# Attention of a hybrid decoder step: sample value products over four column groups, V pages from two queues, logits in pairs

## The chip, the cores and the metric

The kernel runs on one core of a Trainium2 chip. The metric is the device time of one execution in microseconds. A core has TensorE (PE, with its weight loads shown as PEld), VectorE (DVE), ScalarE (ACT), GpSimd (POOL) and SyncE (SP, which here only issues transfers). PSUM is the memory that TensorE writes, in banks of 512 fp32 numbers per partition.

## The reference

One step of a two-layer decoder: 512 prompt tokens and 8 sample tokens share all weights. Layer 0 is a gated MLP mixer, layer 1 is sparse attention, and each is followed by a channel mixer that looks up experts by key. The change touches layer 1's attention alone. In it, every query keeps the best keys by an index score and attends to these only:

```python
def _sparse_attend(q, qi, wi, ki_all, q_pos, n_keep, gather_kv):
    s = jax.nn.relu(jnp.einsum('bthd,bsd->bths', qi, ki_all))
    score = jnp.einsum('bths,bth->bts', s, wi).astype(jnp.float32) * IDX_SCALE
    ...
    _, idx = lax.top_k(score, n_keep)
    k_sel, v_sel = gather_kv(idx)
    logits = jnp.einsum('bthgd,btnhd->bthgn', qg, k_sel).astype(jnp.float32) * (HEAD_DIM ** -0.5)
    ...
    prob = jax.nn.softmax(logits, axis=-1).astype(v_sel.dtype)
    o = jnp.einsum('bthgn,btnhd->bthgd', prob, v_sel)
```

The prompt has 512 keys (16 query heads, 4 KV heads, head dimension 64). Each of the 8 samples has 2048 past keys in 16 pages of 128, found by a page table, and one new key. A V page is 128 rows of 256 fp32 numbers, 128 KB.

## The kernel before

The program has a hand-written instruction stream for each engine, with semaphores between them; nothing is moved by a scheduler. The order in which TensorE's code is written is the order in which it issues.

Attention (`attention` in TensorE's stream, line 789) goes through these stages: projections (line 818), index scores of the prompt (`index_of`, line 834) together with K pages and logits of the samples (line 845), the search for the samples' cutoff (lines 896 to 898, driven by DVE), transposes of the samples' probabilities into `pT_s` and `pnewT` (lines 902 to 910), and then the prompt's attention with the samples' value products between its steps (line 973). Then come the output projection `ao` and the second channel mixer.

The prompt's attention has 64 items, item i being head i % 16 of query block i // 16. Block b has b + 1 blocks of 128 keys. Per item TensorE computes logits (`log_of`, line 936) into one of two banks of `acc`; DVE adds the mask and takes the maximum into `prob` (`biased`, line 2008); ScalarE takes the exponential (`exp_of`, line 1365); TensorE transposes it (`turn`, line 948); ScalarE copies it to `probT` (`take_turned`, line 1373); TensorE multiplies with V (`pv`, line 959); DVE scales the result (`output`, line 2024). TensorE's loop does the logits of item i, the transposes of item i - 2 and the product of item i - 3 in one turn. After the last product of a block, `block_output` (line 968) transposes it, and ScalarE and DVE split it into a high and a low part.

After every odd item there is one value step `s_values(k)` (line 914): sample b, pages 4u to 4u + 3. Its four matmuls have 32 columns of `pT_s` as weights and a page of V as the moving operand (256 columns). Sample b writes partitions 32 (b % 4) to 32 (b % 4) + 31 of one bank, so the four matmuls of a step write the same 32 partitions. After sample b's last step one matmul (line 926) adds the new token's value. There are 32 steps.

SP issues all 128 V pages (line 533), four per buffer `unit`, each after the step that last used the buffer, and reads each page number from `table` into a register. The K pages went through the same four buffers before, issued by SP and ScalarE. Each weight slab of the dense stages is loaded by SP into `raw`, split by ScalarE into `w_hi` and by GpSimd or DVE into `w_lo`. While the prompt's attention runs, GpSimd does nothing; four slabs of `ao` are loaded already.

GpSimd loads the 13 constants of the attention (line 2141) before its part of the norm (line 2083).

## Time and profile before

| | us |
|---|---|
| median of 3 runs | 3879.66 |
| lowest and highest of the 3 | 3871.08 and 3888.6 |
| span of the profiled execution | 3870.3 |
| TensorE busy | 3639.7 |
| VectorE busy | 2458.9 |
| GpSimd busy | 1814.7 |
| ScalarE busy | 1356.3 |

The profile is one execution. Its page gives the busy time of each engine and the costliest groups; the trace behind it can be asked for waits, for the instructions of a stretch in order of time, and for the busy time of each engine and the granted clock of TensorE in a stretch. All times in it are microseconds from the start of the span. An fp32 matmul leaves two records in it, and so does its weight load. Busy times of matmuls overlap, so the distance from one start to the next tells what one costs.

### The profile page before, as it was taken

How to read it: one execution, taken by the hardware profiler on the slowest of the kernel's cores; microseconds unless marked ns; L12 is line 12 of the kernel's file. 1: busy time of each engine (PE TensorE's matmuls, PEld its weight loads, DVE VectorE, ACT ScalarE, POOL GpSimd, SP SyncE). 2: the span in 40 equal slices, each digit the busy share in tenths (PEclk: the TensorE clock that was granted, in tenths of full speed). 3: DMA queues.
4: the chain of work that ended last, by engine and by line, in shares of the span. 5: the costliest groups of instructions: out<-in, count | busy, mean ns of one | idle time of the engine just before them, and what ended most of it. 6: DMA issues, size and time to landing. Idle time of an engine off the chain costs nothing.

```text
span 3870.3 us, 62428 instructions
## 1 busy us (share of the span) xinstructions
PE 3639.7 (94%) x21581; PEld 3432.2 (89%) x21581; DVE 2458.9 (64%) x5408; ACT 1356.3 (35%) x1905; POOL 1814.7 (47%) x1120
## 2 busy tenths in 40 slices
PE   7999999999999999999887698999999999999998
PEld 7998999999999999998853357999999999999998
DVE  2332297777776777874556532297878785777774
ACT  3322243535353333333220233244444444333332
POOL 3433366555655555643520001455555655555551
PEclk9999999999999999999998799999999999999999
DMA  3222267877789999972145131257777788989992
GB/s 120 82 71 72 92 184 251 280 232 284 258 294 275 305 322 314 314 261 90 66 130 161 55 97 45 82 177 232 257 253 258 266 292 268 305 298 334 306 317 99
DMA packets 380011, 812.60 MB, mean 210 GB/s; under 512 B 33544, under 2 KB 239304, under 8 KB 372552
## 3 DMA queue, kind: packets, MB, share of 16 engines
q1 hardware_dynamic: 167024, 464.17, 35.8%
q0 software_dynamic: 61072, 221.08, 16.6%
q10 hardware_dynamic: 151696, 124.51, 10.8%
q8 instruction: 129, 2.11, 0.2%
q14 instruction: 90, 0.74, 0.1%
HBM read 696.90 MB, written 112.74 MB: 209 GB/s over the span
## 4 chain that ended last, share of the span: by engine, by line
PE 72%; DVE 14%; DMA 6%; POOL 2%; issue 2%; ACT 2%; SPq 1%; ACTq 1%; DVEq 0%; POOLq 0%
PE acc L568 43%; PE acc L555 15%; DMA rows<-u_in,expertP 4%; PE misc L699 3%; DVE rows L1654 2%; DMA raw<-slabs_in 2%; PE misc L922 2%; POOL w_lo L2067 1%; PE acc L936 1%; DVE hot_gate L1692 1%; DVE route L1593 1%; DVE misc L1589 1%; PE misc L959 1%; PE misc L578 1%; PE misc L739 1%
## 5 line engine op out<-in xcount | busy, mean ns | idle before, releaser
L2067 POOL TENSOR_TENSOR w_lo<-raw,w_hi 128x1024 fp32r<-128x1024 f32 x368 | 897.9, 2441 | 1336.3 <-ACT w_hi L1017 1335.4
L568 PE MATMUL acc<-h_hi,w_hi 128*128 128x416 f32 x3072 | 1095.6, 357 | 2.5 <-POOL h_lo L2118 1.9
L568 PE MATMUL acc<-h_lo,w_hi 128*128 128x416 f32 x3072 | 1083.9, 353 | 0.0
L568 PE MATMUL acc<-h_hi,w_lo 128*128 128x416 f32 x3072 | 1079.1, 351 | 0.0
L1017 ACT ACTIVATE w_hi<-raw 128x1024 fp32r<-128x1024 f32 x620 | 656.3, 1059 | 1163.3 <-DMA raw<-slabs_in 1124.9
L568 PEld LDWEIGHTS acc<-h_hi,w_hi 128*128 128x128 f32 x3072 | 579.6, 189 | 11.5 <-POOL h_lo L2118 2.6
L568 PEld LDWEIGHTS acc<-h_hi,w_lo 128*128 128x128 f32 x3072 | 580.3, 189 | 7.1
L568 PEld LDWEIGHTS acc<-h_lo,w_hi 128*128 128x128 f32 x3072 | 579.8, 189 | 3.9
L1771 DVE TENSOR_TENSOR w_lo<-raw,w_hi 128x1024 fp32r<-128x1024 f32 x252 | 331.6, 1316 | 199.9 <-ACT w_hi L1017 199.3
L1654 DVE CUSTOM_DVE_ANT_0 rows<-acc,rows 128x1024 f32<-128x1024 f32 (+1 forms) x224 | 273.5, 1222 | 203.2 <-DMA rows<-u_in,expertP 182.0
L568 PE MATMUL acc<-y_hi,w_hi 128*128 128x416 f32 x1024 | 361.1, 353 | 10.5 <-POOL y_lo L2118 5.1
L555 PE MATMUL acc<-h_hi,w_hi 128*128 128x260 f32 x1472 | 307.8, 291 | 58.2 <-DVE h_lo L1438 29.7
L568 PE MATMUL acc<-y_lo,w_hi 128*128 128x416 f32 x1024 | 360.5, 352 | 0.0
L568 PE MATMUL acc<-y_hi,w_lo 128*128 128x416 f32 x1024 | 359.8, 351 | 0.0
L1130 ACT ACTIVATE gelu<-acc 128x416 f32<-128x416 f32 x256 | 132.6, 518 | 641.0 <-PE acc L568 640.8
L2118 POOL TENSOR_TENSOR h_lo<-abuf,h_hi 128x416 fp32r<-128x416 f32 x128 | 206.7, 1615 | 236.3 <-ACT h_hi L1172 235.8
L555 PE MATMUL acc<-h_hi,w_lo 128*128 128x260 f32 x1472 | 300.1, 286 | 0.0
L555 PE MATMUL acc<-h_lo,w_hi 128*128 128x260 f32 x1472 | 299.8, 286 | 0.0
L555 PEld LDWEIGHTS acc<-h_hi,w_hi 128*128 128x128 f32 x1472 | 230.5, 192 | 72.1 <-issue 59.7
L2118 POOL TENSOR_TENSOR y_lo<-abuf,y_hi 128x416 fp32r<-128x416 f32 x112 | 181.4, 1619 | 228.4 <-ACT y_hi L1172 227.9
L1692 DVE TENSOR_SCALAR hot_gate<-misc,idxT,gateT 128x128 f32<-128x128 f32 x832 | 273.8, 400 | 0.0
L1800 DVE TENSOR_TENSOR x<-x,acc 128x416 f32<-128x416 f32 x256 | 148.8, 581 | 132.6 <-PE acc L568 131.9
(331 smaller groups left out, 5347.9 us busy)
## 6 DMA issues: line engine op xcount, KB each, us to landing
raw<-slabs_in SPq DMA_DIRECT2D x620, 512.0 KB, 4.2
act_d<-gelu SPq DMA_DIRECT2D x256, 208.0 KB
gate_d<-gout SPq DMA_DIRECT2D x52, 1024.0 KB, 7.2
abuf<-act_d ACTq DMA_DIRECT2D x32, 1664.0 KB, 11.6
gbuf<-gate_d ACTq DMA_DIRECT2D x30, 1664.0 KB, 23.4
unit<-cv_in SPq DMA_DIRECT2D x128, 128.0 KB, 2.0
unit<-ck_in SPq DMA_DIRECT2D x64, 160.0 KB, 2.9
unit<-ck_in ACTq DMA_DIRECT2D x64, 160.0 KB, 3.1
```

Of the source, the lines that this page charges most:

```text
L555: last = pe.matmul(acc[:, par, half, 0:HT], w[:, c, :], m(c)[:, half * HT:(half + 1) * HT], start=start and c == 0 and w is w_hi[r] and m ...
L568: last = pe.matmul(acc[:, 0, par, 0:ND], w[:, c, :], m(c), start=c == 0 and w is w_hi[r] and m is m_hi, stop=c == KC - 1 and w is w_lo[r])
L699: last = pe.matmul(misc[:, q, j * P:(j + 1) * P], hot1[par][:, t, :], hot_gate[par][:, t, :], start=True, stop=True)
L922: last = pe.matmul(out, pT_s[:, u * UNIT + j, rows], unit[u][:, j, 0:2 * P], start=u == 0 and j == 0, stop=False)
L1017: act.activation(w_hi[r][:], raw[r][:], ACT.Copy).then_inc(hi_done, 1)
L1130: act.activation(gelu[:, par, :], acc[:, 0, par, 0:ND], ACT.Gelu_apprx_tanh).then_inc(acc_free_act, 1)
L1654: dve.tensor_tensor_reduce(out=row, in0=acc[0:n, 1], in1=row, scale=1.0, scalar=0.0, op0=ALU.mult, op1=ALU.add, accum_out=dots[0:n, g, k:k ...
L1692: last = dve.tensor_scalar(hot_gate[par][:, t, :], count_row, idxT[:, 1, t0 + t:t0 + t + 1], gateT[:, t0 + t:t0 + t + 1], ALU.is_equal, AL ...
L1771: dve.tensor_tensor(w_lo[r][:], raw[r][:], w_hi[r][:].bitcast(F32), ALU.subtract).then_inc(lo_done, 1)
L1800: dve.tensor_tensor(x[:, c, D0:TP], x[:, c, D0:TP], acc[:, 0, c % 2, 0:ND], ALU.add).then_inc(acc_free_dve, 1)
L2067: pool.tensor_tensor(w_lo[r][:], raw[r][:], w_hi[r][:].bitcast(F32), ALU.subtract).then_inc(lo_done, 1)
L2118: pool.tensor_tensor(y_lo[par][:, c, 0:ND], abuf[par][:, c, :], y_hi[par][:, c, 0:ND].bitcast(F32), ALU.subtract).then_inc(y_lo_done, 1)
```

## The change

Four parts:

- **Value steps.** `s_values` has 16 steps, numbered s. A step takes two pages of each of four samples (samples 0 to 3 in steps 0 to 7, samples 4 to 7 in steps 8 to 15) and goes round the samples: page 0 of each of the four, then page 1 of each. Neighbouring matmuls write different groups of 32 partitions of the bank. The closing matmuls come four at a time, after steps 7 and 15. A step stands after every fourth item.
- **V pages.** Three buffers `vquad` of eight pages (1 MB) take the place of the four `unit` buffers. In each, SP loads the first page of each sample, and GpSimd the second with an indirect transfer of 128 rows; their row numbers `pageP` are computed once by DVE from `tableB`, the page table on all partitions. Both queues start when the samples' logits are done (`s_new_done`); `vquad` lies where `unit` and `qM` lie.
- **Logits.** `log_of` is called for items i and i + 1 together, at even i, into three banks in turn (`log_bank`: two of `acc`, one of `misc`). The wait for DVE stands before the pair.
- **Order at the start.** The wait for `pnewT` stands before the first logits, not before the first value step. Two more constants are loaded (`rowno`, `tableB`).

```diff
@@ -526,12 +541,16 @@
-                with sp.Fori(0, TS, 1) as b:
-                    for u in range(NU):
-                        sp.wait_ge(unit_used, b * NU + (STEPS + u + 1))
-                        for j in range(UNIT):
-                            sp.dma_start(unit[u][:, j, 0:2 * P],
-                                         a["cv"][bass.ds(page(b, u, j), 1)].squeeze(0)).then_inc(unit_loaded[u], 16)
+                sp.wait_ge(s_new_done, 1)
+                for s in range(VSTAGES):
+                    half, step = divmod(s, VSTEPS)
+                    if s >= VSLOTS:
+                        sp.wait_ge(vquad_used, s - VSLOTS + 1)
+                    for b in range(4):
+                        at_page = (4 * half + b) * PAGES + step * VPAGES
+                        value = sp.value_load(table[0:1, at_page:at_page + 1], min_val=0, max_val=NPOOL - 1)
+                        sp.dma_start(vquad[s % VSLOTS][:, b, 0, :], a["cv"][bass.ds(value, 1)].squeeze(0)).then_inc(
+                            vquad_loaded[s % VSLOTS], 16)
...
@@ -911,29 +930,30 @@
+                def s_values(s):
+
+                    half, step = divmod(s, VSTEPS)
+                    slot = s % VSLOTS
+                    out = [misc[b * 32:b * 32 + 32, 2, half * 2 * P:(half + 1) * 2 * P] for b in range(4)]
+                    rows = [slice((4 * half + b) // 2 * 32, (4 * half + b) // 2 * 32 + 32) for b in range(4)]
+                    pe.wait_ge(vquad_loaded[slot], 16 * 4 * (s // VSLOTS + 1))
+                    pe.wait_ge(vquad_gathered[slot], 16 * 4 * (s // VSLOTS + 1))
+                    for j in range(VPAGES):
+                        for b in range(4):
+                            last = pe.matmul(out[b], pT_s[:, step * VPAGES + j, rows[b]], vquad[slot][:, b, j, :],
+                                             start=step == 0 and j == 0, stop=False)
+                    last.then_inc(vquad_used, 1)
+                    if step == VSTEPS - 1:
+                        for b in range(4):
+                            last = pe.matmul(out[b], pnewT[:, rows[b]], v_tok[0:TS, 4, :], start=False, stop=True)
+                        if half:
                             last.then_inc(s_pv_done, 1)
...
-                    if i >= 2:
-                        pe.wait_ge(log_taken, i - 1)
-                    pe.matmul(acc[:, 0, i % 2, 0:(b + 1) * P], qA[p0:p0 + HD, h // 2, b * P:(b + 1) * P],
+                    pe.matmul(log_bank[i % 3][:, 0:(b + 1) * P], qA[p0:p0 + HD, h // 2, b * P:(b + 1) * P],
...
+                pe.wait_ge(s_pT_done, NU + 1)
                 for i in range(ITEMS + 4):
                     if i >= NHEAD + 3 and (i - 3) % NHEAD == 0:
                         block_output((i - 3) // NHEAD - 1)
-                    if i < ITEMS:
+                    if i % 2 == 0 and i < ITEMS:
+                        if i >= 2:
+                            pe.wait_ge(log_taken, i - 1)
                         log_of(i)
+                        log_of(i + 1)
...
-                    if i % 2 and i < ITEMS:
-                        s_values(i // 2)
+                    if i % 4 == 3 and i < ITEMS:
+                        s_values(i // 4)
...
+                dve.tensor_scalar(pageP[:], tableB[:], float(P), rowno[:, 0:1], ALU.mult, ALU.add).then_inc(pageP_done, 1)
...
+                pool.wait_ge(pageP_done, 1)
+                pool.wait_ge(s_new_done, 1)
+                for s in range(VSTAGES):
+                    half, step = divmod(s, VSTEPS)
+                    if s >= VSLOTS:
+                        pool.wait_ge(vquad_used, s - VSLOTS + 1)
+                    for b in range(4):
+                        k = (4 * half + b) * PAGES + step * VPAGES + 1
+                        pool.indirect_dma_start(out=vquad[s % VSLOTS][:, b, 1, :], out_offset=None,
+                                                in_=a["cv"].rearrange("n p f -> (n p) f"),
+                                                in_offset=bass.IndirectOffsetOnAxis(ap=pageP[:, k:k + 1], axis=0)).then_inc(
+                            vquad_gathered[s % VSLOTS], 16)
```

In the rows that follow, `acc<-kT2,qA` are logits, `acc<-ident,prob` transposes, `misc<-v_tok,probT` products with V, and `misc<-...,pT_s` page matmuls of a value step. TensorE before, items 4 to 7 of block 0:

```order
L936 MATMUL acc<-kT2_153,qA_156 128x128
L948 MATMUL acc<-ident_65,prob2_177 128x128
L959 MATMUL misc<-v_tok_155,probT1_180 128x64
L936 MATMUL acc<-kT2_153,qA_156 128x128
L948 MATMUL acc<-ident_65,prob3_178 128x128
L959 MATMUL misc<-v_tok_155,probT0_179 128x64
L922 MATMUL misc<-unit2_210,pT_s_183 32x256 x4
L936 MATMUL acc<-kT2_153,qA_156 128x128
L948 MATMUL acc<-ident_65,prob0_175 128x128
L959 MATMUL misc<-v_tok_155,probT1_180 128x64
```

TensorE after the change, items 4 to 7 of block 0:

```order
L956 MATMUL acc<-kT2_153,qA_156 128x128
L956 MATMUL misc<-kT2_153,qA_156 128x128
L968 MATMUL acc<-ident_65,prob2_177 128x128
L979 MATMUL misc<-v_tok_155,probT1_180 128x64
L968 MATMUL acc<-ident_65,prob3_178 128x128
L979 MATMUL misc<-v_tok_155,probT0_179 128x64
L956 MATMUL acc<-kT2_153,qA_156 128x128 x2
L968 MATMUL acc<-ident_65,prob0_175 128x128
L979 MATMUL misc<-v_tok_155,probT1_180 128x64
L968 MATMUL acc<-ident_65,prob1_176 128x128
L979 MATMUL misc<-v_tok_155,probT0_179 128x64
L943 MATMUL misc<-vquad1_214,pT_s_183 32x256 x8
```

Two logits now stand together ahead of two rounds of transposes and products, and a value step of eight page matmuls ends four items where two of four page matmuls stood among them.

GpSimd after the change, behind its last work for the projections; before, nothing stood here until the output projection:

```order
L2179 TENSOR_TENSOR qA_156<-rstd_74,rms_h_174 128x520 [waits rrms_done,ra_used]
L2209 DMA vquad0_213<-cv_in,pageP_218 128x256 [waits rrms_used,s_new_done,pageP_done]
L2209 DMA vquad0_213<-cv_in,pageP_218 128x256 x3
L2209 DMA vquad1_214<-cv_in,pageP_218 128x256 x4
L2209 DMA vquad2_215<-cv_in,pageP_218 128x256 x4
L2209 DMA vquad0_213<-cv_in,pageP_218 128x256 [waits vquad_used]
L2209 DMA vquad0_213<-cv_in,pageP_218 128x256 x3
```

The first twelve gathers have no buffer to wait for; from the thirteenth on every four wait for a value step.

## Rows read from the trace of the kernel before

**Rows 1.** The page, part 1: busy time, share of the span, instructions.
```profile
PE 3639.7 (94%) x21581; PEld 3432.2 (89%) x21581; DVE 2458.9 (64%) x5408; ACT 1356.3 (35%) x1905; POOL 1814.7 (47%) x1120
```

**Rows 2.** Waits, 2171 to 2352: who for whom, us in total, times, longest.
```profile
ACT probT L1373 <- PE acc L948: 104.3, 56, 3.6
```

**Rows 3.** Timeline of weight loads, block 0: start, length, instruction, idle before.
```profile
2178.14 0.29 PEld L936 LDWEIGHTS acc<-kT,qA 64*128 64x128 f32 x2 [0.41 <-issue]
2178.56 0.14 PEld L948 LDWEIGHTS acc<-ident,prob 128*128 128x128 f32 x1
...
2179.83 1.43 PEld L922 LDWEIGHTS misc<-unit,pT_s 128*32 128x32 f32 x8
2181.68 0.29 PEld L936 LDWEIGHTS acc<-kT,qA 64*128 64x128 f32 x2 [0.41 <-issue]
...
2185.21 0.13 PEld L926 LDWEIGHTS misc<-v_tok,pnewT 8*32 8x32 f32 x2 [0.41 <-issue]
2185.76 0.29 PEld L936 LDWEIGHTS acc<-kT,qA 64*128 64x128 f32 x2 [0.41 <-issue]
```

**Rows 4.** Stretch of one pair with its value step: busy time of each engine.
```profile
2178.10:2181.65 3.55, 3.55 (x19) 2.11 (x18) 1.58 (x10) 1.51 (x6) 0.00 (x0) 1.00 0.40 111
```

**Rows 5.** Timeline of weight loads: one item's logits in blocks 1, 2 and 3.
```profile
2211.52 0.29 PEld L936 LDWEIGHTS acc<-kT,qA 64*128 64x128 f32 x2 [0.41 <-issue]
2212.14 0.20 PEld L948 LDWEIGHTS acc<-ident,prob 128*128 128x128 f32 x2 [0.33 <-issue]
...
2253.27 0.29 PEld L936 LDWEIGHTS acc<-kT,qA 64*128 64x128 f32 x2 [0.41 <-issue]
2254.11 0.31 PEld L948 LDWEIGHTS acc<-ident,prob 128*128 128x128 f32 x3 [0.55 <-issue]
...
2324.49 0.29 PEld L936 LDWEIGHTS acc<-kT,qA 64*128 64x128 f32 x2 [0.41 <-issue]
2325.55 0.42 PEld L948 LDWEIGHTS acc<-ident,prob 128*128 128x128 f32 x4 [0.76 <-issue]
```

**Rows 6.** Stretches, index scores (line 839) alone: two heads, then one.
```profile
2003.60:2004.70 1.10, 0.92 (x4) 0.30 (x4) 1.00 0.36 122
2000.30:2001.30 1.00, 0.91 (x2) 0.29 (x2) 1.00 0.78 193
```

**Rows 7.** Timeline: the samples' index products on two groups of 64 rows.
```profile
2087.84 0.43 PE L859 MATMUL acc<-unit,qiM 64*64 64x256 f32 x1 [0.60 <-DMA unit<-ck_in]
...
2087.84 0.43 PE L859 MATMUL misc<-unit,qiM 64*64 64x256 f32 x1
...
2088.41 0.19 PEld L864 LDWEIGHTS misc<-unit,qM 128*128 128x128 f32 x1 [0.39 <-issue]
```

**Rows 8.** Timeline of weight loads: change from block 0 to block 1.
```profile
2207.21 0.29 PEld L936 LDWEIGHTS acc<-kT,qA 64*128 64x128 f32 x2 [0.17 <-issue]
2208.91 0.20 PEld L948 LDWEIGHTS acc<-ident,prob 128*128 128x128 f32 x2 [1.41 <-issue]
```

**Rows 9.** Timeline: the start of the 64 items.
```profile
2171.83 0.51 PEld L936 LDWEIGHTS acc<-kT,qA 64*128 64x128 f32 x4 [0.23 <-issue]
...
2172.22 0.25 ACT L1359 ACTIVATE pnewT<-misc 8x128 f32<-8x128 f32 x1
...
2172.66 0.29 DVE L2008 CUSTOM_DVE_ANT_0 prob<-acc,idxs 128x128 f32<-128x128 f32 x1 [4.86 <-PE acc L936]
```

**Rows 10.** Stretch at the start of the items; third from the end: granted clock.
```profile
2171.80:2174.00 2.20, 2.20 (x10) 1.19 (x10) 0.81 (x6) 1.49 (x6) 0.00 (x0) 0.65 0.00 0
```

**Rows 11.** Tile rows: gathers on GpSimd, ns min/median/max, and their landing, us.
```profile
L2110 POOL DMA_INDIRECT rows<-u_in,expertP x192: 933/952/1762, 603.1 to 3199.9; - x192
...
DMA to landing us min/median/max: 3.6/6.0/10.3
```

**Rows 12.** Tile pT_s: weight loads of the value steps, ns.
```profile
L922 PEld LDWEIGHTS misc<-unit,pT_s x256: 106/110/177, 2172.6 to 2344.4; 128*32 128x32 f32 x128
```

**Rows 13.** Timeline of GpSimd: its first operation after the constants' loads.
```profile
1808.34 1.81 POOL L2083 TENSOR_TENSOR h_lo<-sq,h_hi 128x520 fp32r<-128x520 f32 x1 [6.19 <-ACT h_hi L1033]
```

More of the change, by code:

```diff
@@ L117 @@
 OUT = -1.0e30
+VSLOTS, VPAGES = 3, 2
+VSTEPS = PAGES // VPAGES
+VSTAGES = 2 * VSTEPS
 def build(nc, a, outs, layers=2):
@@ L327, in build @@
         table = take("table", [1, TS * PAGES], I32)
+        unit_at = take.end
         unit = [take(f"unit{r}", [P, UNIT, 2 * P + HD]) for r in range(4)]
         qM = take("qM", [P, 2, TS * (P + 16)])
+        v_take = region(unit_at)
+        vquad = [v_take(f"vquad{r}", [P, 4, VPAGES, 2 * P]) for r in range(VSLOTS)]
+        assert v_take.end <= take.end
+        tableB = at("tableB", [P, TS * PAGES], I32, take.end)
         logits = take("logits", [P, SK])
+        pageP = at("pageP", [P, TS * PAGES], U32, ms_at)
+        rowno = at("rowno", [P, 1], F32, take.end - 4096)
         h_take = region(h_at)
@@ L344, in build @@
         misc = es.enter_context(nc.psum_tensor("misc", [P, 4, 512], F32))
+        log_bank = [acc[:, 0, 0], acc[:, 0, 1], misc[:, 3]]
         act_d = [nc.dram_tensor(f"act_d{l}", [NK, P, ND], F32).ap() for l in range(2)]
@@ L394, in build @@
         unit_used = sem("unit_used")
+        vquad_loaded = [sem(f"vquad_loaded{r}") for r in range(VSLOTS)]
+        vquad_gathered = [sem(f"vquad_gathered{r}") for r in range(VSLOTS)]
+        vquad_used, pageP_done = sem("vquad_used"), sem("pageP_done")
         s_new_done, s_relu_done = sem("s_new_done"), sem("s_relu_done")
@@ L436, in build @@
         N_CONST = 10
-        N_ATT = 13
+        N_ATT = 15
         @block.sync
@@ L910, in attention @@
                 pe.transpose(misc[0:TS, 2, 0:P], pnew[:], ident[:]).then_inc(s_ptr_done, 1)
-                def s_values(k):
-                    b, u = divmod(k, NU)
-                    if k == 0:
-                        pe.wait_ge(s_pT_done, NU + 1)
-                    out = misc[b % 4 * 32:b % 4 * 32 + 32, 2, b // 4 * 2 * P:(b // 4 + 1) * 2 * P]
-                    rows = slice(b // 2 * 32, b // 2 * 32 + 32)
-                    pe.wait_ge(unit_loaded[u], 16 * UNIT * (2 * NU + b + 1))
-                    for j in range(UNIT):
-                        last = pe.matmul(out, pT_s[:, u * UNIT + j, rows], unit[u][:, j, 0:2 * P],
-                                         start=u == 0 and j == 0, stop=False)
-                    last.then_inc(unit_used, 1)
-                    if u == NU - 1:
-                        last = pe.matmul(out, pnewT[:, rows], v_tok[0:TS, 4, :], start=False, stop=True)
-                        if b == TS - 1:
+                def s_values(s):
[14 more added lines that the diff above has]
+                        if half:
                             last.then_inc(s_pv_done, 1)
@@ L2007, in biased @@
                         dve.wait_ge(ptr_done, i - 3)
-                    dve.tensor_tensor_reduce(out=prob[i % 4][:, 0:n], in0=acc[:, 0, i % 2, 0:n], in1=idxs[:, b, 0:n],
+                    dve.tensor_tensor_reduce(out=prob[i % 4][:, 0:n], in0=log_bank[i % 3][:, 0:n], in1=idxs[:, b, 0:n],
                                              scale=1.0, scalar=LOW, op0=ALU.add, op1=ALU.max,
@@ L2139, in _ @@
                                  (lane_step, "lane_step"), (lane_sum, "lane_sum"),
-                                 (table, "table")):
+                                 (table, "table"), (rowno, "rowno")):
                     pool.dma_start(dst[:], a[src]).then_inc(att_loaded, 16)
+                pool.dma_start(tableB[:], a["table"][0].partition_broadcast(P)).then_inc(att_loaded, 16)
                 norm(2)
@@ L2273, in layout @@
             "table": np.asarray(i["page_table"]).reshape(1, -1),
+            "rowno": np.arange(P, dtype=f)[:, None],
             "ck": np.concatenate([ck.reshape(NPOOL, P, 2, P).transpose(0, 3, 2, 1).reshape(NPOOL, P, 2 * P),
```

## Prediction

> **What bounds the kernel now.** I read the page first: TensorE is busy for 3639.7 us, 94% of the span of 3870.3, so what counts is whether a stage keeps it as the bound [rows 1]. The diff touches one stage, the 64 items (4 query blocks of 16 heads) of the prompt's attention, with the value products of the eight samples between them. It runs from 2171.83 to 2350.7, 178.8 us. In the list of waits of this stretch the other engines wait for TensorE, ScalarE for 104.3 us for the transposes alone [rows 2]. The timeline of the weight loads gives the rhythm. In block 0 a pair of items with one value step lasts 2178.14 to 2181.68, 3.54 us, with no gap: 0.42 for one item's logits, 0.43 for its transpose and product, the same again, then 1.85 for the value step [rows 3]. In blocks 1 to 3 the pattern is the same with larger pieces, logits up to 1.05 us (2324.49 to 2325.55) [rows 5]. DVE and ScalarE are busy for 1.58 and 1.51 of the 3.55 us of such a pair [rows 4]. So TensorE's issue order is the bound here, and what is taken from it comes off the time until the chain through DVE and ScalarE takes over. Everything after the stage waits for its result, so the saving goes through to the end.
>
> **What a value step costs now, and after.** Four pages are four matmuls of 256 columns onto 32 output partitions, in eight passes (fp32 goes twice through the array). 1.85 us is 8 passes of 0.213 and 0.14 for filling and changing the array's shape [rows 3]. All lie one behind the other since all four write the same 32 partitions. 32 such steps are 59.0 us, and eight closing matmuls against the new token's row take 0.55 each (2185.21 to 2185.76), 4.4 us [rows 3].
> After the change a step has eight pages, two for each of four samples, and the samples lie on four column groups in turn. There are 16 steps. No row of before shows column groups side by side. The nearest row is of row groups: the two 64-row matmuls of the indexer start together at 2087.84 and both, four passes in all, are over by 2088.41: 0.57 = 2 passes of 0.213 + 0.14, not 4 [rows 7]. If the four column groups do the same, a step costs 4 passes + 0.14 = 0.99 us. If nothing overlaps, it costs 16 passes + 0.14 = 3.54. Between them lies a limit by weight loads: one load of 32 columns lasts 0.110 us (median of 256) [rows 12], so 16 of them in single file would make 1.9 with the 0.14. I take 1.2: four-way overlap, and two loads that don't hide. That is nearest to the row-group row, in which the loads hid entirely. Saved: 16 x (2 x 1.84 - 1.2) = 39.7 us. Of the closing matmuls two sets of four are left, 0.65 each: 4.4 - 1.3 = 3.1 saved.
> The value step before shows a load going on behind a running matmul that uses the same 128 rows, for 8 passes of 0.213 fill the 1.84 us with no room for 8 loads. The Trainium skill, TensorE: Matmul & The Clock Gate, section "Part 3: Packing small matmuls", says a load overlaps running matmuls only where the row group differs; the row speaks against that here. By this rule the step would be longer than today's, which is a rival below. The same section gives 2.38 times for three column tiles, not 3; by that ratio the step would be near 1.2.
>
> **Two heads' logits back to back.** Head h lies on partitions 0 to 63 or 64 to 127 by its parity, so two neighbours are two row groups, and the change gives them different banks. The indexer shows exactly this: two heads of 384 columns back to back take 0.92 us in four records (2003.6 to 2004.7), one alone 0.91 in two [rows 6]. The second head is nearly free; I charge 0.08. A single head's logits occupy 0.42, 0.62, 0.84 and 1.05 us in blocks 0 to 3 (load to next load) [rows 3, 5]. Each block has 8 pairs: 8 x (0.34 + 0.54 + 0.76 + 0.97) = 20.9 us. Bounds: 0 if they don't overlap, 23.4 if the second is free.
>
> **What is lost.** (a) Start: the first logits now wait for the copy pnewT, which ends at 2172.47, instead of starting at 2171.83: 0.65. Today the first value step fills the time in which DVE and ScalarE work on items 0 and 1; it now comes two items later, and I charge 0.8 of idle time [rows 9]. The clock is at 0.65 on average over the first 2.2 us, so it rises there from its lower level; with less work it will rise later, 1.0 [rows 10]. (b) Block changes: at 2207.21 the logits run while the transposes wait until 2208.91 for DVE and ScalarE [rows 8]. In the new order the head's logits have been issued before that wait, so it lies bare for 0.62 + 0.84 + 1.05 = 2.5. (c) Block 0: a pair without a value step is 0.42 + 0.08 + 0.86 = 1.36 us on TensorE, less than DVE's 1.58 of busy time (about 1.75 with its gaps) [rows 4]; the next pair, 1.2 longer, absorbs most. 8 pairs x 0.4 = 3.2 at most, 0 at least; I take 1.0. In block 3 a pair is 3.9, far above DVE and ScalarE. (d) DVE's page numbers: one operation on 128x128 elements ahead of the indexer's operands, 0.3 by the 0.29 of another of that size [rows 9]. (e) Two more small loads on GpSimd's queue ahead of the norm: GpSimd idles 6.19 us there, which hides them: 0; bare they would cost the time of two issues [rows 13]. Sum 6.3.
>
> **The moved page loads.** Before, SP issues all 128 V pages; now each engine issues 64, in 16 stages of 1 MB over 3 slots. The first three stages load during the top-k search, more than 60 us before they are needed. For the other 13 GpSimd issues four gathers each. The trace has gathers of 128 rows: 0.95 us to issue, 1.76 at worst, and 6.0 us to landing (10.3 at worst) [rows 11]. A slot has three stage periods, the shortest about 12 us in block 0: 4 x 0.95 + 6.0 = 9.8 fits. SP has nothing else to issue, and the next weight slabs wait for slots that free only after the stage; GpSimd's next subtraction comes after it as well. Charged: 0, as long as the gathers stay at this price.
>
> **The sum.** 39.7 + 3.1 + 20.9 - 6.3 = 57.4 us. The profiled span of 3870.3 would become 3812.9. The span is 9.4 us under the median 3879.66 and 0.8 under the fastest of the three runs (3871.08 to 3888.6), so I take the saving off the median: **3822 us**.
>
> **Rivals.**
> 1. Loads in single file (1.9 us a step): 16 x 0.7 = 11 less saved, 3833. For it: four weight sets must change each 0.4 us, which no row shows. Against: the loads hide in both rows quoted. 0.17.
> 2. Column groups don't overlap at all (3.54 a step, closing matmuls as before): 16 x 2.34 + 3.1 = 40.5 less, leaving 17: 3863. All four would take the same 128 input rows at once, which the row-group pairs don't. 0.10.
> 3. Loads wait for the matmuls of the same rows: 16 x (0.213 + 0.11) + 0.14 = 5.3 a step, 16 x 4.1 + 3.1 = 69 less: 3891, 0.3% slower. This is the skill's rule above worked out; the value step of today speaks against it. 0.03.
> 4. The gathers become the bound, and the kernel gets slower: one mechanism, GpSimd issuing 13 stages of four gathers in the stage. It decides from 13 x 4 x p + 6 = 178.8, so p = 3.3 us per gather; at p = 4.0 the stage takes 214 us and the time is 3915. The measured p is 0.95, so 0.04.
> 5. The logits of two heads don't overlap: 20.9 less, 3843. 0.03.
> 6. The clock stays at its lower level through block 0, where TensorE now has short pauses: some 16 us of work doubled less the pauses, 12 less: 3834. 0.03.
> Forecast: 0.60.
>
> **How the numbers follow.** About 0.5% (19 us) is what a measurement of this kernel can tell from no change. Faster by more than that: the forecast, rivals 1, 5 and 6, and a bit of 4: 0.84. Within: 2 and 3, 0.13. Slower: 0.03. The range: down to 3808 (a step of 0.99 gives 3.4 us, losses of near 0 give 6, and the level of the runs 5), up to 3846 (rivals 1, 5 and 6 with the scatter of the runs). It holds about 0.8; serial column groups lie outside.
>
> **What would show it.** Weight loads of four neighbours starting within 0.1 us and a value step of 1.0 to 1.3 us: the main term. Logits of two items with starts within 0.02 us, and a pair in block 3 of 3.9 us without and 5.1 with a value step: the second. Stage length about 121 us. Waits of the value step for a DMA, or gathers over 2 us: rival 4. If the stage shrinks by 57 and the time doesn't, something behind it (the weight slabs of the output projection) was late; I see nothing that is.

## The result, and the profile after

The changed kernel takes 3850.24 us (median of 4 runs, 3846.35 to 3859.7) against 3875.37 for the kernel before in the same session: ratio 0.9932, 95% interval 0.9911 to 0.9952, about 26 us less. The forecast was 3822, 57 less. It is faster, but less than half of what was forecast came, and the time lies above the range.

TensorE's share of the span is 93% of 3844.5, against 94% of 3870.3 [rows 1], and GpSimd has the gathers on top. The page of the changed kernel, part 1:

```profile
PE 3594.2 (93%) x21581; PEld 3414.4 (89%) x21581; DVE 2455.4 (64%) x5409; ACT 1358.1 (35%) x1905; POOL 1873.4 (49%) x1186
```

**The two new forms do what was hoped.** The timeline of TensorE in block 3 of the changed kernel (start, length, instruction):

```profile
2300.90 0.69 PE L956 MATMUL acc<-kT,qA 64*128 64x512 f32 x1
2300.91 0.69 PE L956 MATMUL misc<-kT,qA 64*128 64x512 f32 x1
...
2301.96 0.65 PE L968 MATMUL acc<-ident,prob 128*128 128x128 f32 x4
...
2304.67 1.07 PE L943 MATMUL misc<-vquad,pT_s 128*32 128x256 f32 x16
2305.67 0.70 PE L956 MATMUL acc<-kT,qA 64*128 64x512 f32 x2
```

Two heads' logits start 0.01 apart and both are over by 2301.96: 1.06 us for two where [rows 5] has 1.05 for one. A value step of eight pages takes 1.00 us (2304.67 to 2305.67), sixteen weight loads included, where before four pages took 1.85 [rows 3]. That is 4 passes of 0.213 and 0.14, the lower bound of the prediction.

**But the stage takes 146 us, not 121.** In the stretches by block of the changed kernel (busy time of each engine; then granted clock, DMA share, GB/s):

```profile
core 0: us, PE busy (x) PEld busy (x) DVE busy (x) ACT busy (x) POOL busy (x), PEclk, DMA share, GB/s
2173.90:2202.70 28.80, 25.91 (x154) 15.56 (x154) 13.65 (x89) 12.64 (x55) 15.08 (x16) 0.62 0.45 125
2202.70:2242.60 39.90, 31.88 (x209) 21.14 (x209) 16.06 (x82) 15.46 (x49) 15.25 (x17) 0.75 0.39 119
2242.60:2283.00 40.40, 33.77 (x250) 22.65 (x250) 18.09 (x82) 19.36 (x51) 15.17 (x16) 0.87 0.36 108
2283.00:2320.10 37.10, 34.74 (x300) 26.16 (x300) 17.32 (x73) 20.41 (x46) 3.79 (x4) 1.00 0.11 30
sum 146.20, PE 126.30 PEld 85.51 DVE 65.12 ACT 67.87 POOL 49.30; mean PE 31.57 PEld 21.38 DVE 16.28 ACT 16.97 POOL 12.32
```

Two things are new. The granted clock is 0.62, 0.75 and 0.87 in blocks 0 to 2, that is, long stretches at the lower of the two levels (0.50); before, it was full from some 2 us after the start [rows 10, 4]. And TensorE idles for 19.9 us (146.2 - 126.3) though it has more than enough to do. Block 3, where GpSimd has only four gathers left, is at the full clock with 2.4 us of idle time.

The stage is 32.8 us shorter than before (146.2 against 178.95), the span only 25.8. Ahead of the stage 2.1 us are lost and behind it 4.9. These parts differ from run to run: when the same kernel was profiled again (e18), the stage began at 2185.6 instead of 2173.9. So single spans compare to some 10 us only; the stage's own length and the medians are the better measures.

What it idles for is in the list of waits, 2174 to 2310 (engine, line, waited for: total, times, longest):

```profile
DVE o_tok L2049 <- remote: 16.4, 11, 2.4
ACT probT L1397 <- remote: 10.1, 5, 2.7
DVE prob L2033 <- remote: 3.6, 4, 1.1
```

DVE and ScalarE wait 30 us in sum for something that the profile can give to no engine ("remote"). Before, there is no such row: ScalarE waits for TensorE's transposes [rows 2]. The timeline around one of these pauses, all engines:

```profile
2219.20 0.95 POOL L2209 DMA_INDIRECT vquad<-cv_in,pageP  x1 [4.72 <-PE misc L943]
...
2220.46 0.95 POOL L2209 DMA_INDIRECT vquad<-cv_in,pageP  x1 [0.30 <-issue]
...
2221.71 0.95 POOL L2209 DMA_INDIRECT vquad<-cv_in,pageP  x1 [0.31 <-issue]
...
2222.19 0.56 PE L979 MATMUL misc<-v_tok,probT 128*128 128x64 f32 x4
...
2222.58 0.39 PE L968 MATMUL acc<-ident,prob 128*128 128x128 f32 x2
...
2222.96 0.95 POOL L2209 DMA_INDIRECT vquad<-cv_in,pageP  x1 [0.30 <-issue]
...
2224.84 0.39 ACT L1397 ACTIVATE probT<-acc 128x256 f32<-128x256 f32 x1 [2.67 <-remote]
2224.97 0.28 DVE L2049 TENSOR_SCALAR o_tok<-misc,rinv 128x64 f32<-128x64 f32 x1 [1.63 <-remote]
...
2225.28 0.66 PE L979 MATMUL misc<-v_tok,probT 128*128 128x64 f32 x4 [2.31 <-ACT probT L1397]
```

TensorE's product is over at 2222.75 and its transposes at 2222.97. DVE, which waits for the one, and ScalarE, which waits for the other, both go on only at 2224.8 to 2225.0, and TensorE, which waits for ScalarE, at 2225.28. What the two have in common is that they wait for a signal of TensorE, and that a row of four gathers is under way on GpSimd. In eleven of the 13 rows of gathers in this trace such a wait ends during the row or within 2.1 us of the start of its last gather; in the last 25 us of the stage, behind all of them, there is none. The name is given by inference: some waits that end at the same moments of a row are listed under TensorE.

### The profile page after: what moved, and what is told of

Its sections match the earlier page's. It is cut to its first block, busy times and chain, and to the rows that moved or that the text cites. A ratio compares the mean times of both kernels' runs of the same rounds, so it can differ in the third digit from the quotient of the medians.

```text
span 3844.5 us, 61950 instructions
## 1 busy us (share of the span) xinstructions
PE 3594.2 (93%) x21581; PEld 3414.4 (89%) x21581; DVE 2455.4 (64%) x5409; ACT 1358.1 (35%) x1905; POOL 1873.4 (49%) x1186
## 4 chain that ended last, share of the span: by engine, by line
PE 69%; DVE 16%; DMA 5%; issue 4%; ACT 2%; POOL 2%; ACTq 0%; SPq 0%; another core or an unknown queue 0%; DVEq 0%; POOLq 0%
PE acc L587 42%; PE acc L574 15%; PE misc L718 3%; DMA rows<-u_in,expertP 3%; DVE rows L1678 2%; DMA raw<-slabs_in 2%; DVE hot_gate L1716 1%; POOL w_lo L2092 1%; PE misc L979 1%; DVE route L1617 1%; DVE misc L1613 1%; ACT w_hi L1041 1%; PE misc L758 1%; PE misc L597 1%; PE acc L968 1%
```

## The experiments

All ratios are to the kernel before, run beside them. "Stage" is from the first logits to the end of the last turned block, in the profiled run; "idle" is that time less TensorE's busy time. Stage, idle and clock are of the one profiled run, which need not be a middle one: of e12 it is 8 us under the median, of e3 the slowest of ten and 24 us over it, of e15 the fastest of ten and 11 us under it.

| kernel | ratio (95% interval) | stage us | idle us | mean clock |
|---|---|---|---|---|
| before | 1 | 178.9 | 4.4 | 1.00 |
| changed | 0.9932 (0.9911 to 0.9952) | 146.2 | 19.9 | 0.82 |
| changed again (e18) | 0.9942 (0.9924 to 0.9961) | 149.4 | 19.3 | 0.81 |
| e1 SyncE issues all pages | 0.9892 (0.9876 to 0.9909) | 132.3 | 13.1 | 0.86 |
| e2 all pages by gathers | 1.0033 (1.0020 to 1.0047) | 195.2 | 53.6 | 0.72 |
| e3 gathers, single logits | 1.0007 (0.9986 to 1.0027) | 193.8 | 3.7 | 0.64 |
| e4 value steps in halves | 0.9912 (0.9895 to 0.9928) | 148.5 | 21.9 | 0.83 |
| e5 before + pairs of logits | 0.9970 (0.9958 to 0.9983) | 165.2 | 9.2 | 0.96 |
| e6 SyncE, single logits | 0.9977 (0.9944 to 1.0010) | 158.7 | 4.2 | 0.81 |
| e7 before + gathers in twos | 0.9996 (0.9986 to 1.0007) | 180.1 | 4.6 | 0.99 |
| e8 changed + fill | 0.9920 (0.9903 to 0.9937) | 144.1 | 25.4 | 0.88 |
| e9 SyncE + fill | 0.9883 (0.9862 to 0.9904) | 131.2 | 15.2 | 0.90 |
| e10 e9 + earlier start | 0.9893 (0.9874 to 0.9912) | 133.0 | 15.6 | 0.88 |
| e11 gathers in twos | 0.9890 (0.9868 to 0.9912) | 140.2 | 16.1 | 0.83 |
| **e12 GpSimd, plain DMAs** | **0.9864 (0.9835 to 0.9893)** | **115.3** | **8.0** | **0.97** |
| e13 e12 + fill + earlier start | 0.9851 (0.9828 to 0.9873) | 115.7 | 7.5 | 0.96 |
| e14 gathers in ones | 0.9896 (0.9865 to 0.9928) | 138.5 | 10.7 | 0.78 |
| e15 e12, single logits | 0.9977 (0.9942 to 1.0012) | 149.4 | 4.0 | 0.86 |
| e16 before + gathers in fours | 1.0026 (1.0011 to 1.0040) | 187.4 | 6.8 | 0.96 |
| e17 all pages GpSimd, plain | 0.9897 (0.9881 to 0.9914) | 137.7 | 18.1 | 0.86 |

Two theories stood at the start. **G**: the gathers hold the other engines up, and the pauses keep the clock down. **C**: the new order on TensorE by itself lets the clock fall; the gathers are innocent.

**Gathers away, gathers doubled (e1, e2).** e1 gives GpSimd's pages to SyncE, e2 SyncE's to GpSimd.

```diff
@@ sync, in the loop over the four samples (e1) @@
+    value1 = sp.value_load(table[0:1, at_page + 1:at_page + 2], ...)
+    sp.dma_start(vquad[s % VSLOTS][:, b, 1, :], a["cv"][bass.ds(value1, 1)]...)
@@ gpsimd @@
-    pool.indirect_dma_start(out=vquad[s % VSLOTS][:, b, 1, :], ...)
```

> SyncE issues both V pages of every sample, 8 direct DMAs a stage, and GpSimd issues none; TensorE's order and all else are those of the changed kernel. Theory G (the gathers hold DVE and ScalarE up, once per stage for 1.5 to 2.5 us, and these pauses keep the clock down): the waits of ScalarE and DVE that end by nothing on an engine are gone, the granted clock of 2220 to 2280 is 1.00, the stage goes from 146 to 120 to 127 us and the time from 3850 to 3825 to 3832. Rival C (the clock stays down because of the new order on TensorE: an empty start and denser work between short gaps; the gathers are innocent): pauses or not, the clock in the stage's first 50 us stays at 0.5 to 0.7, the stage is 140 us or more and the time within 6 us of 3850.

> GpSimd issues both V pages of every sample, 8 gathers a stage, SyncE none. Theory G: the pauses double, 20 to 30 us more in the stage (166 to 176 us), time 3870 to 3880. Rival C: no change, within 6 us of 3850; 13 stages of 8 gathers at 1.25 us are 130 us, which fits into the stage, so the issue rate alone adds little (0 to 10 us).

Without gathers no wait has a remote releaser, and the stage is 14 us shorter. But the clock was still low (0.60 in the first 15 us, 0.69 and 0.77 at two later ones), and a new wait came, on which I had not reckoned: SyncE needs 1.10 us for a page, 8.8 for a stage of eight, and TensorE waits for pages. The wait of e1:

```profile
PE misc L946 <- DMA vquad<-cv_in: 5.4, 3, 3.8
```

With twice the gathers the pauses are not doubled but more than tripled, up to 9.8 us each, and here GpSimd pauses too. The waits of e2:

```profile
ACT probT L1387 <- remote: 61.6, 14, 9.8
DVE prob L2023 <- remote: 25.1, 6, 7.9
DVE o_tok L2039 <- remote: 20.0, 8, 4.7
```

One of these pauses in e2's timeline of all engines:

```profile
2189.40 0.27 PE L946 MATMUL misc<-kT,qA 64*128 64x128 f32 x1
...
2192.21 0.95 POOL L2205 DMA_INDIRECT vquad<-cv_in,pageP  x1 [0.30 <-issue]
2194.87 0.29 DVE L2023 CUSTOM_DVE_ANT_0 prob<-misc,idxs 128x128 f32<-128x128 f32 x1 [6.81 <-remote]
2194.95 0.28 ACT L1387 ACTIVATE probT<-acc 128x128 f32<-128x128 f32 x1 [6.80 <-remote]
2195.06 0.94 POOL L2199 DMA_INDIRECT vquad<-cv_in,pageP  x1 [1.91 <-remote]
```

The logits for which DVE waits were over at 2189.67; DVE starts on them 5.2 us later, together with ScalarE and GpSimd, all three of which wait for signals of TensorE. So G holds for the pauses; for the clock it was not enough.

**TensorE's order (e3, e4, e6).** e3 and e6 issue the logits one at a time, with gathers and with SyncE alone; e4 cuts each value step in two.

```diff
@@ tensor, e3 and e6 @@
-    if i % 2 == 0 and i < ITEMS:
+    if i < ITEMS:
         if i >= 2: pe.wait_ge(log_taken, i - 1)
         log_of(i)
-        log_of(i + 1)
@@ tensor, e4 @@
-    if i % 4 == 3: s_values(i // 4)
+    if i % 2: s_values(i // 4, [i // 2 % 2])
```

> The logits are issued one item at a time as in the kernel before (a wait for DVE before each, three banks kept); value steps and gathers are those of the changed kernel. By the sum of the prediction the pairs are worth 20.9 us with the clock full. Theory G and C alike: if TensorE is the bound in blocks 1 to 3, the time rises by 15 to 21 us to 3865 to 3871. If the stalls and the clock set the end instead, part of the pairs' worth is lost already and the time rises by under 10. With more work on TensorE the clock could also rise earlier (rival C), which would take back up to 10 us.

> Each value step is cut in two: the four matmuls of the first pages after one pair of items, the four of the second pages after the next, so that TensorE's work is spread evenly and the first of it comes two items earlier. Theory G: within 5 us of 3850, the pauses stay. Rival C: the clock is full earlier in block 0 (0.9 and more in 2177 to 2200 instead of 0.6), the stage shortens by 10 to 20 us, time 3830 to 3840.

> Round robin alone: SyncE issues all V pages, the logits go one item at a time, no gathers. Sum of the prediction: 42.8 less some 4 us of losses, 39 us saved, ratio 0.990, if the clock is full. The same with gathers stayed at clock 0.50 for 130 us and had a ratio of 1.0007. Theory G (the gathers keep the clock down): clock full by 2200 and a stage of 140 to 145 us. Theory C (the order and thinner work of TensorE keep it down): clock 0.50 for most of the stage again, 180 to 194 us, ratio 0.997 to 1.001.

e4 changed nothing that can be measured. e3 lost far more than the pairs' worth, and by neither theory's path: it has no waits named remote (idle 3.7 us) though it has the same 13 rows of four gathers, TensorE is busy throughout, and still the clock stands at 0.50 for some 130 us. Two stretches of e3:

```profile
2244.60:2259.60 15.00, 15.00 (x62) 9.57 (x65) 4.93 (x26) 4.75 (x17) 3.79 (x4) 0.50 0.23 72
...
2334.60:2349.60 15.00, 14.34 (x94) 9.49 (x94) 6.88 (x26) 7.45 (x18) 3.79 (x4) 1.00 0.25 72
```

e6, without gathers, was at 0.50 for 60 us. The single runs of these two kernels lie 35 and 56 us apart, those of e15, which has the same order, 50, and those of all others 5 to 24, as they would if the moment of the rise were a matter of chance. So with round robin steps and single logits the clock can stay down for long although TensorE is busy. Why, when it rose within 2 us in the old order [rows 10], is not in these traces.

**The parts alone, on the old order (e5, e7).** e5 is the kernel before with pairs of logits in three banks and nothing else; e7 the kernel before with two of each step's four pages by gathers.

> The kernel before with one edit: the logits of two heads back to back in three banks. V pages, value steps and the start are those of before, with no gathers. Sum of the prediction: 20.9 us less and 2.5 lost at block changes, 18 us saved, ratio 0.9953, the stage from 178.9 to about 160, the clock full from 2174 on. Theory C (any thinning of TensorE's work lets the clock fall): the clock shows stretches at 0.50 also here, and the saving is under 10 us.

> The kernel before with TensorE's order untouched; of every value step two of the four V pages come by gathers of GpSimd, 64 in all, two per step (with the page numbers on DVE and the two small loads). Theory G: DVE and ScalarE pause here as well; with TensorE full of work a part of each pause is covered, 5 to 25 us more than before (ratio 1.001 to 1.006), and if gathers by themselves hold the clock down, far more (up to 80). Theory C: the same time as before within 3 us and a clock of 0.97 or more over the stage.

e5 saved 13.8 us of the stage and 12 of the time, not 18. TensorE's busy time fell by 18.6 (20.9 expected): in block 2 the pairs gave 5.4 (6.1 expected), and there were three dips of the clock to 0.89 over 15 us. Its idle time rose by 4.8. Of these 2.5 are the charge for the block changes, and it was right: TensorE's waits there were 2.5 us before and are 5.0 in e5. Another 1.4 are two waits for V pages, which I had not expected. The waits of the kernel before, then of e5:

```profile
PE acc L948 <- DVE h_lo L2033: 2.5, 3, 1.0
...
PE acc L947 <- DVE h_lo L2035: 5.0, 3, 1.7
PE misc L923 <- DMA unit<-cv_in: 1.4, 2, 0.9
```

e7 was the surprise for G: 56 gathers in the stage, no pause, the clock at 0.99. It fell so far as it said that gathers hold the others up wherever they stand. What differs is that e7 issues them two in a row, every 3.5 us in block 0 and every 6.8 in block 3.

**Fill ahead of the stage (e8), and with SyncE's pages (e9, e10).** Before the stage TensorE waits 10.4 us for the samples' softmax. The fill puts eight unused 128x512 products there.

```diff
+    for f in range(8):
+        pe.matmul(misc[:, 1, :], ident[:], v_tok[:, 0:2, :], start=True, stop=True)
     pe.wait_ge(s_prob_done, 2)
```

> The changed kernel with 8 unused 128x512 matmuls on TensorE in the 10.4 us in which it waits for the samples' softmax (after the last digit of the top-k search, ahead of the sixteen transposes), so that the clock is full when the stage starts. If the start's low clock is what is lost: block 0 at 1.00 instead of 0.5 to 0.7, 8 to 12 us less, time about 3840 and the stage about 134. If the pauses and gaps inside the stage let the clock fall whatever it was at the start: the clock is back at 0.50 within 20 us and the time is within 4 us of the changed kernel.

> The changed kernel with both causes treated: SyncE issues all V pages (no gathers), and the 8 unused matmuls before the stage bring the clock up. If the pauses from the gathers and the clock are the whole of what the forecast missed, the clock is 1.00 from the first item on (with dips of one window at most at the block changes), the stage takes the predicted 121 to 124 us, and the ratio is 0.986 to 0.987 (some 51 to 55 us saved). If the clock still falls in block 0 or 1, where TensorE now has gaps, the stage is 128 to 132 and the ratio 0.988 to 0.989, as without the fill.

> The same with the start of before: the first two logits ahead of the wait for the new token's row, and each value step two items earlier (after items 1, 5, 9 ...), so that TensorE has work while DVE and ScalarE do items 0 and 1. The prediction charged 0.65 + 0.8 for that; 1 to 2 us less than the run without it, stage 119 to 122. If it is the clock in block 0 that decides, the fuller start keeps it up and the gain is larger, up to 6.

The fill raised the clock in the first 15 us from 0.61 to 0.89 and saved 2 us of the stage: TensorE's busy time fell by 7.6 us, and its idle time rose by 5.5, to 25.4. With the pauses in place a faster TensorE waits for them. In e9 the clock was 1.00 for 30 us and then fell (0.56, 0.76, 0.77), where TensorE was waiting for SyncE's pages (7.2 us in five waits). In e10 it was 1.00 for 15 us and then 0.66 to 0.86, and nothing was gained. Expected were 121 to 124 us; SyncE's 8.8 us a stage forbid that, which I should have seen in e1.

**The length of a row of gathers (e11, e14, e16).** In e11 GpSimd waits for TensorE to be two items further after every second gather, in e14 for the next item before each, in e16 the old order gets its gathers in fours.

```diff
@@ gpsimd, e11 (e14: if b, and + 1 + b) @@
     for b in range(4):
+        if b == 2 and s >= VSLOTS:
+            pool.wait_ge(pv_done, 4 * (s - VSLOTS) + 3)
@@ gpsimd, e16, once for two steps of the old order @@
-    pool.wait_ge(unit_used, b * NU + (STEPS + u + 1))
+    if u % 2 == 0 and j == 1: pool.wait_ge(unit_used, b * NU + (STEPS + u + 2))
```

> The changed kernel; GpSimd issues the four gathers of a stage as two and two, the second two only when TensorE is two items further. If the pauses come from a row of gathers (their descriptors or packets holding up TensorE's signals until the last of them is out), they shrink or vanish as in the old order with gathers in twos, where there were none: waits of ScalarE and DVE without a releasing engine under 8 us instead of 30, 4 to 10 us less, time 3840 to 3846. If they come from TensorE's denser order with gathers of any spacing, they stay at 25 to 35 us in sum and the time stays at 3850.

> The changed kernel; GpSimd waits for TensorE's next item product before each gather, so that no two gathers follow one another where TensorE is the slower. Row theory (pauses come only in rows of three or more gathers 1.25 us apart): no pauses at all, stage 115 to 125, ratio 0.986 to 0.988, the same as with plain DMAs. Density theory (gathers of any spacing hold the denser order up): waits without a releasing engine stay at 10 us or more and the ratio is 0.989 or above.

> TensorE's old order, half the V pages by gathers, issued four in a row every second value step instead of two every step. Row theory: DVE and ScalarE now pause in the old order too, once for each row (28 rows, 0.5 to 2.5 us each), of which TensorE covers a part; 5 to 30 us slower than with gathers in twos (ratio 1.001 to 1.008). Density theory: no pauses, ratio 0.999 to 1.001.

In e11 the rows at first still had four gathers, since TensorE was ahead of GpSimd. Up to 2220 there are pauses, the last of them behind a row that starts at 2214.18:

```profile
2210.80 0.38 ACT L1397 ACTIVATE probT<-acc 128x256 f32<-128x256 f32 x1 [3.03 <-remote]
...
2219.85 0.38 ACT L1397 ACTIVATE probT<-acc 128x256 f32<-128x256 f32 x1 [2.47 <-remote]
```

From 2222 on the gathers lie in twos, and not one of the remaining 28 has a pause. e14 shows nearly the same: its waits named remote lie behind rows of three, but for one of 0.6 us, which ends 1.5 us after the start of a single gather (2191.28), itself 2.0 us behind a row of three. e16 is the other direction: in fours the gathers cost the old order 7.3 us of the stage and some 12 of the time (1.0026 against 0.9996, the intervals don't overlap). Of the 7.3 us 5.2 are TensorE's busy time at a lower clock and 2.1 its idle time. Only one wait there is named remote (0.3 us), but the rows show the same late signals under TensorE's name. One of them in e16's timeline:

```profile
2282.30 0.78 PE L976 MATMUL misc<-v_tok,probT 128*128 128x64 f32 x6
...
2282.70 0.95 POOL L2200 DMA_INDIRECT unit<-cv_in,pageP  x1 [0.30 <-issue]
...
2284.63 0.28 DVE L2042 TENSOR_SCALAR o_tok<-misc,rinv 128x64 f32<-128x64 f32 x1 [1.78 <-PE misc L976]
```

The product is over at 2283.08, and DVE starts on it 1.55 us later, 1.9 us after the start of the row's last gather. There are seven such starts in e16's stage, 0.5 to 1.7 us late, each 0.5 to 0.6 or 1.9 to 2.1 us after the start of a row's last gather. In e7, with gathers in twos, there is none.

So the length of the row decides, in either order. A row of four is not enough by itself, though. In e3 (single logits) DVE starts late once behind 13 such rows: at 2345.99, 1.2 us after the product's end, behind the last row, which lies at clock 1.00. In the changed kernel rows at a low clock had pauses too, so the clock alone doesn't explain e3; what does is open. That e14 is not faster than e11 is the clock again: 0.53 and 0.50 from 2220 to 2250 with TensorE busy for 13 of 15 us.

**The form of the transfer (e12, e17).** GpSimd issues its pages as plain DMAs, the page number in a register, as SyncE does. Queue, bytes and packets stay as they were.

```diff
-    pool.indirect_dma_start(out=vquad[s % VSLOTS][:, b, 1, :], out_offset=None, in_=..., in_offset=...pageP[:, k:k + 1]...)
+    value = pool.value_load(table[0:1, k:k + 1], min_val=0, max_val=NPOOL - 1)
+    pool.dma_start(vquad[s % VSLOTS][:, b, 1, :], a["cv"][bass.ds(value, 1)].squeeze(0))
```

> The changed kernel; GpSimd issues its 64 pages as plain DMAs with the page number in a register instead of gathers by 128 row numbers. If it is the indirect form that holds the others up, the pauses are gone and the time is near that of SyncE alone (ratio about 0.989). If any transfer of GpSimd's queue does it, they stay (ratio 0.992 to 0.993).

> GpSimd issues both V pages of every sample as plain DMAs, 8 a stage, SyncE none: the counterpart of the 8 gathers a stage, which made the stage 195 us long and the ratio 1.0033. Form theory (only the indirect form holds the others up): no pauses; GpSimd issues one page each 1.14 us, 9.1 us a stage, as SyncE alone did at 1.10, so TensorE waits for pages in the shorter blocks as there: stage 130 to 137, ratio 0.988 to 0.990. Traffic theory (GpSimd's queue at twice the rate): pauses as with the gathers, 150 us or more, ratio 0.993 or above.

This was the missing piece. The blocks of e12, same columns as above:

```profile
2176.20:2196.80 20.60, 18.90 (x155) 11.64 (x155) 13.45 (x89) 12.80 (x55) 6.98 (x13) 0.92 0.52 154
2196.80:2222.20 25.40, 23.31 (x209) 15.94 (x209) 16.01 (x82) 15.51 (x51) 10.08 (x19) 1.00 0.66 194
2222.20:2254.90 32.70, 30.56 (x250) 21.35 (x250) 18.13 (x82) 19.00 (x51) 8.71 (x17) 0.95 0.46 136
2254.90:2291.45 36.55, 34.44 (x300) 26.12 (x300) 17.39 (x73) 20.35 (x46) 2.15 (x4) 1.00 0.12 36
sum 115.25, PE 107.21 PEld 75.05 DVE 64.99 ACT 67.67 POOL 27.91; mean PE 26.80 PEld 18.76 DVE 16.25 ACT 16.92 POOL 6.98
```

Against the changed kernel 31.0 us less: 19.1 of TensorE's busy time, which is the clock (the same 912 matmuls), and 11.9 of its idle time, which is the pauses. No wait is remote. GpSimd is even quicker at it, so the edit changes two things at once, the form of the transfer and the time for which it keeps GpSimd busy:

```profile
2182.25 0.54 POOL L2210 DMA_DIRECT2D vquad<-cv_in  x1 [62.07 <-issue]
2183.39 0.54 POOL L2210 DMA_DIRECT2D vquad<-cv_in  x1 [0.60 <-issue]
2184.52 0.54 POOL L2210 DMA_DIRECT2D vquad<-cv_in  x1 [0.59 <-issue]
```

0.54 us each and 1.14 apart, sixteen in an unbroken row (2182.25 to 2199.30), with no pause. So a long row by itself does no harm, nor does the traffic. e17 settles that: 104 plain DMAs, where 104 gathers made 195 us, make 138, with no pause, and what TensorE waits for are the pages (GpSimd needs 9.1 us for eight):

```profile
PE misc L933 <- DMA vquad<-cv_in: 10.6, 7, 3.9
```

It is the indirect form, three or more in a row, that holds the others up; whether by what it sends or by the 0.95 us for which it keeps GpSimd busy isn't told apart.

**What is left, and the best version (e13, e15, e18).**

> GpSimd's plain DMAs and round robin value steps, logits one item at a time: what the round robin is worth without pauses. Sum of the prediction 42.8 less 4 of losses, or 178.8 - 39 = 140 us for the stage, ratio 0.990, and the pairs worth 20 to 25 us (115 against 140), if the clock is full. If the clock stays at 0.50 as it did with gathers (for 130 us) and with SyncE alone (for 60 us), the cause of the low clock is the single logits with round robin steps themselves: stage 160 to 190, ratio 0.997 to 1.001.

> GpSimd's plain DMAs, the 8 unused matmuls before the stage, the first two logits ahead of the wait and the value steps two items earlier. With the clock full from the first item (0.89 over the first 15 us before, some 3 us at the lower level) and the start filled: stage 110 to 113 instead of 115, ratio about 0.985 to 0.986. If the earlier value steps make TensorE wait for pages, or the clock falls in the gaps of block 0, it is 115 to 120 and the ratio 0.986 to 0.988.

> The changed kernel, not edited: ratio 0.991 to 0.995 as measured first, stage 143 to 150, waits of ScalarE and DVE without a releasing engine of 20 to 35 us in sum, each in or just behind a row of three or more gathers, none where GpSimd is at rest, and a granted clock of 0.75 to 0.88 over the stage. If the pauses lie elsewhere in this second trace, or the clock is full, my reading of the first one was of a single run.

e15 stood at clock 0.50 for 35 us and then near full in its fastest run, the one profiled; its other runs took up to 50 us more. Two stretches:

```profile
2188.30:2203.30 15.00, 15.00 (x70) 9.42 (x71) 5.98 (x37) 4.80 (x23) 3.97 (x9) 0.50 0.48 141
...
2233.30:2248.30 15.00, 13.73 (x103) 8.35 (x102) 7.43 (x32) 7.41 (x20) 3.12 (x7) 1.00 0.34 107
```

No gathers, no gap, and the clock down: that part of theory C is left over, for the order with single logits. Its blocks 2 and 3, at full clock, take 38.1 and 42.7 us against 49.9 and 52.1 before, so the round robin is worth 11.8 and 9.4 us a block, and e12's 32.7 and 35.5 between the same marks make the pairs worth 5.4 and 7.2 on top. e13 adds nothing that the intervals can tell from e12 (the fill gives a clock of 1.00 in the first 15 us, a dip to 0.77 follows). e18 repeats the changed kernel: 149 us, clock 0.81, waits with remote releasers of 19 us for DVE and ScalarE in 12 cases, again each in or up to 2.1 us behind the last start of a row of four gathers. The first trace was no exception. The version to keep is e12: 3821.49 us (3813.42 to 3831.24), against 3877.08 for the kernel before beside it.

## Why the prediction was wrong

- **The value step** (forecast 1.2 us, bounds 0.99 and 3.54): 1.00 at full clock, 1.87 at half (2183.57 to 2185.44). The term was 3 us too small. All weight loads hide. The Trainium skill, TensorE: Matmul & The Clock Gate, section "Part 3: Packing small matmuls", has loads overlap only where the row group differs, and gives 2.38 times for three column tiles. Here all sixteen loads go to the same 128 rows and hide, and a page costs 0.125 us against 0.46, 3.7 times less.
- **The pairs of logits** (20.9 less 2.5 at the block changes): the single pair as forecast, 1.06 for two of block 3. The 2.5 at the block changes was right as well: the waits there rose from 2.5 to 5.0 (5.0 in e12 too). Alone on the old order 13.8 of the expected 18.4 came; dips of the clock and waits for V pages took most of the rest.
- **The moved page loads, "Charged: 0, as long as the gathers stay at this price"**: this step failed. The gathers stayed at 0.95 us and 1.25 apart, and no value step waited for a page. But I had asked only whether the pages come in time and whether GpSimd is free, not what a gather does to others while it is issued. [rows 11] shows that gathers occur elsewhere in the kernel, and I took their price from there. Their neighbours would not have shown the harm either: of the 448 gathers in the trace of before 372 stand alone and 76 in twos, none in a row of three or more (starts under 1.45 us apart), and no wait in the whole trace is named remote. What had no row was four of them 1.25 us apart, and I took that to cost the same. With the form exchanged (e12) the stage is 115 us and the median 3821.5.
- **The clock, "rises later, 1.0"**, and rival 6 (lower level through block 0, 12 us, chance 0.03): this failed too, and with it 19 of the 31 us. It was low in parts of blocks 0 to 2. The pauses have a share in it: with plain DMAs and the same order the mean is 0.97. Whether the new order has one too is open: with single logits it leaves the clock down for long where nothing else disturbs it (e15), but the changed kernel has pairs. How the 19 us divide is not shown. A higher clock alone would not have saved them: e8 raised the mean to 0.88 with the pauses in place and got 2 us for it. No run puts the fill ahead of single logits.
- **Rivals 1, 2, 3 and 5** are out by the rows of block 3. **Rival 4** named the right instruction and the wrong mechanism: a rate of 3.3 us per gather as its threshold, where the harm came at 0.95.
- The losses at the start were near the charge: 0.6 us for the wait, and nothing gained where it was taken out (e10, e13).
- The sum itself was sound: in e12 TensorE's busy time is 67.3 us less than before where 63.7 were forecast, and its idle time 3.6 more where the losses were put at 6.3. The stage takes 115 us instead of 121, in a run that lies 8 us under e12's median. By the medians 53 us came where 57 were forecast.

## What to carry to other kernels

Before work moves to another engine's queue, ask not only whether that queue has the time, but what its instructions do to the signals of others: look for a stretch of the trace in which they stand as densely as they will and run beside the engines concerned. The price of single instructions says nothing of a row of them. If there is no such stretch, try the move in two forms before you trust it. Where the page numbers are known as scalars, a plain DMA with a register offset costs GpSimd 0.54 us instead of 0.95 and left the others alone here; where a gather is needed, keep to two in a row. And a gain on the bounding engine is paid out only as long as its clock stays up: read the granted clock by block before and after.

## What was not expected of the hardware

- Rows of three or more gathers (128 rows of 1 KB each, 0.95 us, 1.25 apart) can hold up what waits for TensorE's signals, with waits of up to 3.8 us with four in a row (e4) and 9.8 with eight (e2). With four the last wait ends at most 2.3 us after the start of the row's last gather, with eight at most 2.9, but for one row with 3.8. Two in a row did nothing, in either order, and in e3 rows of four did next to nothing. By what path a gather does this is open: in the stage the instruction queues moved 17 packets in the changed kernel and 19 in e12, which has no pauses, and the data queue carried the same bytes and packets in both. The Trainium skill, SBUF — State Buffer, section "Who interferes with whom", says of SBUF's ports that "DMA never contends with a compute engine" and that "PE and ACT never wait on anyone". For plain DMAs these traces agree; with rows of gathers ScalarE stood for up to 9.8 us. Whether by a port or by another path these runs don't tell.
- The granted clock can stay at 0.50 for 35 to 130 us while TensorE's records are without a gap but for the block changes (15.00 us of 15.00; e3, e6, e15), and rise in the midst of the same pattern of work.
- Four column groups of fp32 matmuls run fully side by side, loads included, at either clock.
